# Reordering the head of two expert layers: the first expert's scaled tokens before the token weights

## The reference, cut to what matters

```python
g_prob = jax.nn.softmax((xf @ w_group).astype(jnp.float32), axis=-1)
...
top_p, top_i = lax.top_k(jax.nn.softmax(e_logits, axis=-1), MOE_TOP_K)
top_p = top_p / jnp.sum(top_p, axis=-1, keepdims=True)
weight = (g_gate[:, None] * top_p).reshape(A)
...
def expert_block(args):
    xb, e = args
    h = jax.nn.silu(xb @ w_gate[e]) * (xb @ w_up[e])
    return h @ w_down[e]
```

## Time and profile before

| what | value |
|---|---|
| median of three runs | 2209.25 us |
| lowest and highest run | 2206.16 and 2212.03 us |
| the profiled execution's own time | 2209.27 us |
| its span (first to last instruction) | 2207.4 us |
| PE busy | 1869.4 us (85%) |
| DVE busy | 725.0 us (33%) |
| ACT busy | 381.1 us (17%) |
| DMA | 565.20 MB, 256 GB/s over the span |

### The profile page before, as it was taken

The page is one execution under the profiler, slowest core; times in us unless marked ns, Lnnn a source line. Parts: engine busy times, 40 slices in busy tenths (PEclk is TensorE's granted clock), DMA queues, the critical chain, the costliest instruction groups (busy, mean ns, idle before and its releaser), DMA issues.

```text
span 2207.4 us, 31562 instructions
## 1 busy us (share of the span) xinstructions
PE 1869.4 (85%) x12745; PEld 1171.1 (53%) x12745; DVE 725.0 (33%) x2426; ACT 381.1 (17%) x1032; POOL 86.6 (4%) x92
## 2 busy tenths in 40 slices
PE   8999998667666699887766766798999999899998
PEld 7686555334333344454433443444688644468863
DVE  4354353122122314542222222457222114732211
ACT  2122111011111112311111111214221001422100
POOL 0112100000000010000000000000001000000110
PEclk9999999788888899899888888899999999999999
DMA  9333369999999953379999999942344344224420
GB/s 346 117 113 115 130 269 426 424 424 425 425 425 424 402 215 114 123 306 424 426 425 423 425 425 424 367 156 74 124 153 154 128 156 153 77 86 153 153 96 19
DMA packets 112375, 565.20 MB, mean 256 GB/s; under 512 B 12456, under 2 KB 15726, under 8 KB 79470
## 3 DMA queue, kind: packets, MB, share of 16 engines
q1 hardware_dynamic: 112238, 563.21, 64.1%
HBM read 562.14 MB, written 1.05 MB: 255 GB/s over the span
## 4 chain that ended last, share of the span: by engine, by line
PE 65%; DMA 22%; issue 6%; DVE 4%; ACT 3%; SPq 0%; DVEq 0%; ACTq 0%
DMA ring<-in_moe_w_gate_dram 15%; PE ps L2466 14%; PE ps L1666 11%; PE ps L296 9%; PE ps L689 8%; PE ps L1232 5%; DMA arena<-in_moe_w_gate_dram 4%; PE ps L1338 3%; PE ps L1242 2%; PE ps L729 2%; DMA ring<-in_moe_w_up_dram 2%; PE ps L2007 1%; ACT arena L1803 1%; PE ps L782 1%; PE ps L481 1%
## 5 line engine op out<-in xcount | busy, mean ns | idle before, releaser
L689 PE MATMUL ps<-ring,arena 128*32 128x256 f32 x2816 | 220.6, 482 | 160.2 <-issue 134.9
L2466 PE MATMUL ps<-arena,ring 128*128 128x256 f32 (+1 forms) x1536 | 305.5, 362 | 0.0
L2466 PEld LDWEIGHTS ps<-arena,ring 128*128 128x128 f32 x1536 | 271.9, 190 | 33.9 <-issue 1.0
L689 PEld LDWEIGHTS ps<-ring,arena 128*32 128x32 f32 x2816 | 122.4, 137 | 253.0 <-issue 227.4
L1666 PE MATMUL ps<-ring,arena 128*128 128x512 f32 (+1 forms) x576 | 251.8, 596 | 3.7 <-DVE arena L421 3.7
L296 PE MATMUL ps<-ring,arena 128*128 128x512 f32 x480 | 207.6, 593 | 0.8 <-ACT arena L2309 0.8
L705 DVE TENSOR_TENSOR arena<-arena,ps 64x256 f32<-64x256 f32 x64 | 27.2, 425 | 499.1 <-ACT arena L699 499.0
L1666 PEld LDWEIGHTS ps<-ring,arena 128*128 128x128 f32 x576 | 110.2, 193 | 136.7 <-issue 136.4
L689 PE MATMUL ps<-arena 128*32 128x256 f32 x1280 | 98.4, 474 | 66.2 <-issue 66.2
L2526 DVE SCALAR_TENSOR_TENSOR arena<-ps,pcol,arena 128x255 f32<-128x255 f32 (+1 forms) x176 | 84.9, 482 | 210.8 <-ACT arena L2499 207.6
L296 PEld LDWEIGHTS ps<-ring,arena 128*128 128x128 f32 x480 | 90.7, 190 | 112.3 <-issue 111.0
(11 more groups left out here) (308 smaller groups left out, 1965.2 us busy)
## 6 DMA issues: line engine op xcount, KB each, us to landing
ring<-in_moe_w_gate_dram SPq DMA_DIRECT2D x44, 2048.0 KB, 33.8
ring<-in_moe_w_up_dram SPq DMA_DIRECT2D x44, 2048.0 KB, 38.3
ring<-in_moe_w_down_dram SPq DMA_DIRECT2D x44, 2048.0 KB, 38.6
ring<-in_w_up_dram SPq DMA_DIRECT2D x22, 2048.0 KB, 7.9
arena<-in_moe_w_gate_dram SPq DMA_DIRECT2D x20, 2048.0 KB, 33.6
arena<-in_moe_w_up_dram SPq DMA_DIRECT2D x20, 2048.0 KB, 38.1
arena<-in_moe_w_down_dram SPq DMA_DIRECT2D x20, 2048.0 KB, 38.3
ring<-in_ssm_w_in_dram SPq DMA_DIRECT2D x12, 2048.0 KB, 9.9
```

Of the source, the lines that this page charges most:

```text
L689: mm = nc.tensor.matmul(ps[j * CAP:(j + 1) * CAP, 5, 0:256], xg[:, b, (k % 2 * 4 + k // 2) * CAP:(k % 2 * 4 + k // 2 + 1) * CAP], w[:, k, ...
L2466: mm = nc.tensor.matmul(ps[:, n % 4, lo:hi], w[:, k, k4 * P:(k4 + 1) * P], xT_mlp[:, k, lo:hi], start=(k == 0), stop=(k == KD - 1))
```

## The change

In `experts_act`, the copy of expert 0's picked tokens comes before the exponentials. In `experts_dve`, `dve_weights` leaves the place between expert 0's slots and expert 0's scaled tokens and goes into the first expert, behind expert 1's slots and ahead of the tally. No instruction is added or taken away, and the programs of PE and SP are untouched. The order on DVE becomes: slots 0, scaled tokens 0, slots 1, weights, tally, hidden 0. The order on ACT becomes: copy 0, exponentials, silu 0. Both expert layers use this code.

```diff
@@ -929,9 +929,8 @@
             def experts_act(act):
+                step_pick_copy(act, m, lambda s: s.at(1), None, 0)
                 head.act_exps(act)
-
-                step_pick_copy(act, m, lambda s: s.at(1), None, 0)
 
                 def expert(q, i):
@@ -982,6 +981,7 @@
                         step_slots(dve, m, v1, prev1, 1 - i % 2, e1)
                     if first_quad(q) and i == 0:
+                        head.dve_weights(dve)
                         head.dve_tally(dve)
                     step_hidden(dve, m, v, prev, i % 2)
@@ -992,7 +992,6 @@
                 step_slots(dve, m, lambda s: s.at(1), None, 0, 0)
-                head.dve_weights(dve)
                 step_xg(dve, m, lambda s: s.at(1), None, 0)
                 for i in range(4):
```

## The result

| | before | after |
|---|---|---|
| median, five runs each | 2207.79 us | 2198.39 us |
| lowest and highest | 2206.16 and 2212.03 | 2194.28 and 2200.31 |
| ratio after / before | | 0.995, 95% interval 0.9935 to 0.9965 |
| profiled execution, span | 2207.4 us | 2192.3 us |

The change makes the kernel faster, by 9.4 us of the medians. One of the eleven executions of `e12` took 4756 us and is left out of its ratio.

A forecast was written before the change was run, and what follows sets the result against it. The prediction took the expert layers to be bound by an unbroken weight stream starting when the first gate/up product ends. 2209.25 - 2.9 (earlier starts) - 3.3 (clock) = 2203.1 us, range 2199.0 to 2208.5.

The forecast's parts named there:

- The start of the gate/up product sets the layer's stream: Both expert layers' heads: first gate/up product starts 1.44 us earlier, so the weight stream does too; together 2.9 us.
- Both moves are needed, and the moved work is covered: Heads: copy gives 0.42, weights 1.02; moved DVE work, 3.7 us, hides in the tally wait with 1.4 to spare.
- its sum of the two parts (0.42 and 1.02): Each head: ACT's earlier copy gives 0.42 us, DVE's weights behind the scaled tokens 1.02; together 1.44.
- The clock in the heads: First gate/up products: less idle keeps PE's clock up in most executions; 1.65 us per head, 3.3 for both.
- comes later and costs as much: Rival, heads: starts move 1.44 earlier, but the low clock returns as often or later at equal cost; 2206.4 us, chance 0.22.
- whatever brings that product's end forward by x brings the end of the layer forward by x: Expert layers: one unbroken weight stream starts at the first gate/up product's end, so its gain reaches the layer's end.
- hardly anything that happens inside the layer counts: Expert layers, between the first gate/up product's end and the stream's end: work there hardly affects the time.
- a slower one: Rival, layers' ends: low clock hits the eight-matmul combinations, 3.7 us more each, 7.3 together; 2213.7 us, chance 0.08.
- an unchanged 401.9 from the gate issue to the last down issue: Sign, SP's issues: the span from expert 3's gate weights to the last down weights should stay 401.9 us.
- The baseline: Whole kernel before the change: median of the runs 2209.25 us, from which the forecast's gains were subtracted.

The follow-up runs named there:

- e12: The kernel before, unchanged, run a third time for another profile of its heads and layer ends; ratio to before 0.9992 (0.9982 to 1.0001).
- e7: After, with DVE repeating a tiny subtraction 13 times ahead of the first expert's scaled tokens; ratio to before 1.0001 (0.9992 to 1.0009).
- e14: After, with DVE repeating a tiny subtraction 15 times ahead of the first expert's scaled tokens; ratio to before 1.0003 (0.9994 to 1.0011).
- e4: Before, with only ACT's copy moved ahead of the exponentials, DVE's order kept; 2210.43 us against 2207.7, ratio 1.0014.
- e6: Before, with two 128x512 matmuls put into PE's idle stretch behind the turn in each head; 2203.64 us against 2207.38, ratio 0.9987.
- e9: After, with three 128x512 matmuls on PE ahead of the wait for the last expert's weights; 2195.99 us against before's 2208.97, ratio 0.9942.

## Why the prediction was right and where it was wrong

- **The start of the gate/up product sets the layer's stream**: right. It was forecast 1.44 earlier in each head, and came 1.42 earlier. With the order of after and about the start of before (e7, e14), the gain is gone.
- **Both moves are needed, and the moved work is covered**: right. The weights were forecast to end 1.4 before the tally and end 1.3 before it; silu's table load was forecast 0.3 before the product's end, and was 0.4. The copy alone is a loss (e4), which the prediction did not price, though its sum of the two parts (0.42 and 1.02) reads as if each stood alone.
- **The clock in the heads**: right for the product, 3.66 in all of after's, but not because the clock stayed up. In both heads of after's first profile the low clock came right behind it, in expert 0's down product (3.59 and 3.55 in place of 1.93). The prediction had "comes later and costs as much" as a rival; it came later and cost nothing. That was not forecast, so the term came in by luck as far as the reason goes. The term was 3.3 for both heads. Three profiles of before lost 4.15, 1.69 and 1.48 there, mean 2.4, so it was 0.9 high. e6 gained 2.9 (interval 0.9 to 4.6) by time, with a part of it at the layers' ends.
- **The step that failed** is "whatever brings that product's end forward by x brings the end of the layer forward by x", and with it "hardly anything that happens inside the layer counts". The sum had the clock at the layers' ends at nothing, and the only rival on it was a slower one. Its mechanism was there, with the other sign. From the gate issue to the last combination, before took 887.6, 888.0 and 887.6 over both layers, and after 885.6 and 885.7: 2.1 us. The stream kept its length, as forecast: in 33 of the 34 layers profiled the last product starts 432.1 to 432.6 behind the gate issue. What changed is the last product itself: in before's three profiles it took 6.40 to 6.58 in five layers and 5.35 in one, in after's two it took 5.35 in all four. In before's first layer the down product behind it was slow too (3.17). The prediction named the very row, the last product at 6.40, and that it could fall to 3.66; it left it out of the sum. Its own sign for this, an unchanged 401.9 from the gate issue to the last down issue, came out at 400.97 and 401.07. In numbers: 2.84 (start) + 2.44 (heads' clock) + 2.08 (ends) = 7.4, which is what the layers' sums differ by, and within the repeated ratio's 4.9 to 10.4 us.
- **The baseline** of 2209.25 was the median of three runs. Later sets of before gave 2207.4 to 2209.0, and the repetition of after, at 2199.27, lies inside the forecast's range. The first comparison's 9.4 is 2 us more than the 7.4 that the layers account for; its repetition gave 8.1. What the stretches outside the layers do varies from execution to execution (first pick at 303.4 and 307.9 in after's two profiles), and I take the remainder as this scatter, which the intervals allow but don't prove.
- The Trainium skill, "TensorE: Matmul & The Clock Gate", Part 1, says that the count of slow matmuls varies from run to run and advises against fitting to it. The first half agrees with the runs (4.97, 5.35 and 5.14 in one and the same product). Its reason for the second half, that the loss is under 1% of a usual span, holds here too: 4.5 us are 0.2%. But the change is worth only 0.34%, and these 4.5 us are most of its 7.4.

**Still open.** Why the ends are long with the gate issue at 9.3 to 10.2 behind the pick, and short ahead of that and behind it, was not worked out. The start of the stream doesn't settle it alone: with the gate issue 8.5 behind the pick one end was short and three were long, and e6 has one of each. Shown is that the ends change with the delay while the order is kept, and that the last product's clock goes with them: up to 5.35 in all short ends, 6.1 or more in all long ones. The product before it goes the other way in all 28: it took 5.51 to 6.54 ahead of a short end and 5.02 to 5.45 ahead of a long one. What decides on which of the two the low clock falls longer is not shown. The timed runs confirm the ends' 2.1 us only within their intervals of some 2 us to either side.

## What to carry to other kernels

When a stream of transfers waits for one product, look at what each engine's order puts ahead of that product, and move all of it: one engine's part alone can be a loss, because the other then waits for what was pushed back. A shorter idle stretch of TensorE can be worth more than its length: the product ran at full clock in all ten heads with at most 1.20 us of idle ahead of it, and in three of eighteen with 1.78 or more. Look also at where the low clock goes then, since a slow product costs only where something waits for it. Price the clock from several profiles of the same kernel, not from one. And where TensorE waits for the last transfer of a stage, filling that wait with matmuls can save what the low clock costs behind it (2.9 us over two layers in e9's profile).

## What was unexpected in the hardware

- A step: 0.59 us more of delay ahead of the product cost 6.8 us over two layers in the profile (899.8 to 906.7) and 4.2 by the timed ratios, as the low clock came back in both first products (5.35 and 5.26) and the last products slowed down some 430 us later.
- A layer whose weights stream at 424 to 427 GB/s without a gap still changed its end by 1 to 2 us with the clock in its last product, and three matmuls ahead of it took 2.9 us off both layers.
- With the product earlier, the low clock moved from it to expert 0's down product (3.59 in place of 1.93) and cost nothing there. At the layers' ends the same trade shows between the last two gate/up products: 6.41 and 5.35 in after, 5.26 and 6.40 in before.
- Three profiles of one program differ by 4.1 us at the first pick (304.81 to 308.87) before any of the changed code has run.
